# Attention values with rounded parts: 128-column products, and the halves added at the output

## The chip, the cores and the metric

The kernel runs on one core of one Trainium2 chip. The metric is the device time of one execution in microseconds (us). Engines are named as the profile names them: PE (matrix products), PEld (its weight loads), DVE (vector), ACT (scalar and functions), POOL (GpSimd), SP (here only DMA issue).

## The reference, cut to what matters

Two blocks of a network on 512 tokens of width 1024, all in float32: a block with a state-space branch, an attention branch and an MLP, then a gated-MLP layer and a second attention layer. Both attention layers are banded, with 16 query heads of width 64 on 4 key/value heads, blocks of 128 queries, and a sink logit per head. In the first a query block sees the block before, its own and the next (384 keys), in the second the block before and its own (256 keys):

```python
m = max(logits.max(-1), sink)
p = exp(logits - m)
out = (p @ v) / (p.sum(-1) + exp(sink - m))
```

## The kernel before, in words

The weights come as 66 panels of 1024 x 512 (P_... numbers a panel, O_... its output). Each is split into a rounded part w_hi (ACT, `make_hi`, L259) and the rest w_lo (POOL, L263), both of type float32r; activations are split in the same way, and a product of float32 accuracy is three float32r products: hi by hi, hi by lo, lo by hi. `main_step` (L300) gives, for one k of 8 and each m of four banks mb[m], these three products of 512 columns. At k = 0 it waits, bank by bank, until the result of the panel before has been taken from mb[m] (semaphore `bank_free`).

The attention (class `Attention`; att1 with 384 keys, att2 with 256) runs underneath such panels. Each has two halves, j = 0 and 1, of eight heads t = 0 to 7 with four query blocks c = 0 to 3. A half is a query panel (`query_panel`, which makes q and k parts and the logits of head 0), then the gate panel, during which the heads are worked off: in `heads`, step (t, m) of PE is

- before its main products: `pe_turn_p` (L789), the transposes of the probabilities of head t-1, block m, into an aux bank (ab),
- the three main products of k = t, bank m,
- after them: `pe_values` (L802), probabilities by values of head t-1, block m, into ab[3]; then `pe_logits` (L772 and L773) of head t+1, block m.

A block c has two or three key blocks of 128 in att1 (2, 3, 3, 2) and one or two in att2 (1, 2, 2, 2). Each is one product for values, of type float32, which the chip does in two instructions. The logits of a head go alternately to ab[0] and ab[1]; those of head 0 have other banks in att1.

The other engines follow in written order. ACT: `act_turned` (L880) copies the turned probabilities from the aux bank to SBUF (pt), `act_exp` (L850) makes probabilities from lg to pr, one sink exp a head (L854), one `make_hi` a head. DVE: `dve_logits` (L819) adds the bias and takes the maximum, from the logit bank to lg; `dve_den` (L889, L891) makes the reciprocal of the denominator; `dve_out` (L897) multiplies ab[3] by it into o (o1 or o2) and signals `att_out`, for which the next head's first values wait.

Where a half ends, DVE takes the four banks of the gate panel (L2162 in att1: adds the gate bias into gt; L2280 in att2: copies to zt), each signalled with bank_free, and then does den and out of head 7. On PE, head 7's turn and values are four steps of their own in att1 (`attention`), without main products between them. In att2 they lie in k = 0 of the next panel (`last_head`, and for j = 1 the output panel P_BO, line 1937). Two more things hang on output 7 in att2: DVE's gate (L2285, L2287) makes the final o, and `op_o2` (L372) transposes it on PE, under the next query panel after k = 3 for j = 0, and under P_BO after k = 2 for j = 1. `ch` is a chain on DVE: the instruction signals its end and DVE waits for that.

Of the kernel before, what the change touches and what calls it, by code (L numbers as in the profile page):

```python
# [18 lines left out]
F32 = mybir.dt.float32  # L19
# [72 lines left out]
def two_blocks(nc, d, out):  # L92
    ctx = ExitStack()
    with ctx:
# [70 lines left out]
        v_sb = at("v_sb", R0 + 24 * KB, [P, NT, 256])  # L165
# [11 lines left out]
        pr = [at("pr0", B0 + 18 * KB, [P, NT, 384]), at("pr1", B0 + 48 * KB, [P, NT, 384])]  # L177
        pt = [at("pt0", R0 + 20 * KB, [P, 384]), at("pt1", R0 + 22 * KB, [P, 384])]
        lg2 = [at("lg2a", B0 + 12 * KB, [P, NT, 256]), at("lg2b", B0 + 20 * KB, [P, NT, 256])]
        pr2 = [at("pr2a", B0 + 16 * KB, [P, NT, 256]), at("pr2b", B0 + 24 * KB, [P, NT, 256])]  # L180
# [494 lines left out]
        v_turned, v_in = sem("v_turned"), sem("v_in")  # L675
# [3 lines left out]
        p_turned, p_in, values, att_out = sem("p_turned"), sem("p_in"), sem("values"), sem("att_out")  # L679

        class Attention:
# [3 lines left out]
            def __init__(self, i, width, o, sink, lg, pr):  # L685
                self.lg, self.pr = lg, pr
# [22 lines left out]

            def act_v(self, eng):  # L710
                for j in range(2):
                    eng.wait_ge(v_turned, self.b + j + 1)
                    eng.activation(v_sb[:, :, j * P:j * P + P], ab[j][:, :].rearrange("p (c n) -> p c n", c=NT),
                                   ACT.Copy).then_inc(v_in, 1)
# [37 lines left out]
            def pe_logits(self, eng, j, t, c, og):  # L752
# [7 lines left out]
                if t == 0 and self.w == 384:  # L760
                    if c == 0:
                        eng.wait_ge(biased, one_up(j * 32 + self.b * 32))
                        eng.wait_ge(p_in, one_up(j * 32 + self.b * 32))
                        eng.wait_ge(att_out, one_up(j * 8 + self.b * 8))
                elif c >= 2 or t > 0:
                    eng.wait_ge(biased, one_up(n - 1))
                else:
                    eng.wait_ge(biased, one_up(j * 32 + self.b * 32))
# [6 lines left out]
            def logit_bank(self, t, c):  # L775

                return ab[c if t == 0 and self.w == 384 else c % 2]

            def turned_bank(self, t, c):

                return ab[1 if t == 7 and c % 2 else 2]

            def pe_turn_p(self, eng, j, t, c):
# [3 lines left out]
                eng.wait_ge(p_in, one_up(n - 1 if t == 7 and c else n))  # L787
                for b in range(nb):
                    x = eng.transpose(self.turned_bank(t, c)[:, b * P:b * P + P], self.pr[t % 2][:, c, off + b * P:off + b * P + P], ident)  # L789
                x.then_inc(p_turned, 1)  # L790

            def pe_values(self, eng, j, t, c):
                half = t // 4
                n = j * 32 + (self.b * 32 + t * 4 + c)
                lo, nb, off = self.span(c)
                if c == 0:
                    if t == 0:
                        eng.wait_ge(v_in, self.b + 2)
                    eng.wait_ge(att_out, one_up(j * 8 + (self.b * 8 + t)))
                eng.wait_ge(p_in, one_up(n + 1))  # L800
                for b in range(nb):
                    x = eng.matmul(ab[3][:, c * HP:c * HP + HP], pt[c % 2][:, b * P:b * P + P],  # L802
                                   v_sb[:, lo + b, bass.ds(j * P + half * HP, HP)],
                                   start=(b == 0), stop=(b == nb - 1))
                x.then_inc(values, 1)

            def dve_logits(self, eng, j, t, cs=range(NT)):
                for c in cs:
# [3 lines left out]
                    if c == 0:  # L812

                        eng.wait_ge(exp_done, one_up(j * 32 + (self.b * 32 + max(t - 1, 0) * 4)))
                        if t >= 2:
                            eng.wait_ge(sink_exp, j * 8 + (self.b * 8 + t - 1))
# [23 lines left out]
            def act_exp(self, eng, j, t, cs):  # L840
# [3 lines left out]
                if 0 in cs:  # L844
                    eng.wait_ge(den_done, one_up(j * 8 + (self.b * 8 + max(t - 1, 0))))
                    eng.wait_ge(values, one_up(j * 32 + (self.b * 32 + max(t - 1, 0) * 4)))
# [1584 lines left out]
```

## Time and profile before

| | |
|---|---|
| median of 3 runs | 1859.57 us (1858.75 to 1859.9) |
| the profiled execution's own time | 1861.01 us |
| its span | 1859.1 us |
| busy in the span | PE 97%, DVE 45%, ACT 46%, POOL 45% |
| att1: query panels and heads | about 562 to 741 us from the start |
| att2: query panels and heads | about 1641 to 1815 us |

The span is what the trace covers, from the first to the last instruction; the time holds in addition what lies around it. Starts in the rows are us from the start of the span. In a timeline row stand the start, the duration, engine, line, operation, output<-input, the shape and how many were merged, then in brackets the idle time before it and who ended it. Matmuls are pipelined: the duration of one overlaps the next, so two starts are compared, not durations.

### The profile page before, as it was taken

The page shows a single profiled execution, that of the slowest core. Times are in us where ns is not written, and L with a number is a line of the kernel's source. Part 1 is how long each engine was busy: PE and PEld are TensorE (multiplying, and loading weights), DVE is VectorE, ACT ScalarE, POOL GpSimd, SP SyncE. Part 2 cuts the span into 40 slices and gives each one's busy share as a digit, 9 for nine tenths or more (in the row PEclk, how much of TensorE's full clock was granted, in tenths as well). Part 3 has the DMA queues.
Part 4 walks back from the last instruction along what each step waited for, and adds up shares of the span by engine and source line. Part 5 has one row for each costly group of instructions (what it writes and reads, how often), then busy time and mean ns, then how long its engine had stood idle before and what let it go on. Part 6 is the DMA issues. An engine that isn't in the chain of part 4 may idle for free.

```text
span 1859.1 us, 26998 instructions
## 1 busy us (share of the span) xinstructions
PE 1810.3 (97%) x9064; PEld 1505.4 (81%) x9064; DVE 832.6 (45%) x1384; ACT 848.2 (46%) x1795; POOL 834.8 (45%) x598
## 2 busy tenths in 40 slices
PE   8999999999999999999999999999999999999998
PEld 7788888887888888888888888877888888887776
DVE  4688888888304443235430033050253311534644
ACT  4655555554325655324442244253533332456652
POOL 4654555577353132435444444445454444442322
PEclk9999999999999999999999999999999999999999
DMA  5732121222133121423233333324232223221211
GB/s 175 138 90 69 56 68 56 60 64 57 57 102 120 52 79 51 132 89 102 83 98 102 91 102 91 102 81 159 81 108 80 85 86 102 80 71 57 63 40 57
DMA packets 46223, 159.85 MB, mean 86 GB/s; under 512 B 4763, under 2 KB 7195, under 8 KB 45884
## 3 DMA queue, kind: packets, MB, share of 16 engines
q1 hardware_dynamic: 38592, 140.53, 24.7%
q10 hardware_dynamic: 7548, 18.20, 4.0%
q8 instruction: 54, 0.88, 0.2%
q14 instruction: 29, 0.24, 0.0%
HBM read 152.42 MB, written 6.29 MB: 85 GB/s over the span
## 4 chain that ended last, share of the span: by engine, by line
PE 81%; DVE 8%; issue 4%; ACT 4%; POOL 1%; DMA 1%; DVEq 0%; ACTq 0%; POOLq 0%
PE main L300 60%; PE main L328 4%; PE aux L802 4%; PE aux L656 2%; PE main L1800 2%; PE aux L789 2%; DVE u_acc L2002 1%; PE aux L772 1%; PE aux L372 1%; DVE x_res L564 1%; PE aux L773 1%; DVE y_all L2080 1%; PE aux L1888 1%; PE aux L647 1%; ACT w_hi L259 1%
## 5 line engine op out<-in xcount | busy, mean ns | idle before, releaser
L263 POOL TENSOR_TENSOR w_lo<-raw,w_hi 128x512 fp32r<-128x512 f32 x504 | 700.7, 1397 | 895.0 <-ACT w_hi L259 883.1
L259 ACT ACTIVATE w_hi<-raw 128x512 fp32r<-128x512 f32 x486 | 304.5, 630 | 696.7 <-PE main L300 683.7
L300 PE MATMUL main<-w_hi,a_hi 128*128 128x512 f32 x736 | 304.2, 413 | 2.3 <-ACT vv L1547 1.5
L300 PE MATMUL main<-w_hi,a_lo 128*128 128x512 f32 x736 | 288.1, 391 | 0.0
L300 PE MATMUL main<-w_lo,a_hi 128*128 128x512 f32 x736 | 287.3, 390 | 0.0
L300 PE MATMUL main<-a_hi,w_hi 128*128 128x512 f32 x576 | 231.2, 401 | 1.6 <-ACT u_raw L1296 1.6
L300 PE MATMUL main<-a_hi,w_lo 128*128 128x512 f32 x576 | 225.2, 391 | 0.0
L300 PE MATMUL main<-a_lo,w_hi 128*128 128x512 f32 x576 | 224.9, 390 | 0.0
L300 PEld LDWEIGHTS main<-w_hi,a_lo 128*128 128x128 f32 x736 | 138.1, 188 | 30.3
L300 PEld LDWEIGHTS main<-w_hi,a_hi 128*128 128x128 f32 x736 | 138.5, 188 | 28.4 <-ACT vv L1547 1.9
L300 PEld LDWEIGHTS main<-w_lo,a_hi 128*128 128x128 f32 x736 | 138.8, 189 | 23.0
L300 PE MATMUL main<-w_hi,f_hi 128*128 128x512 f32 x352 | 138.6, 394 | 1.5 <-DVE f_lo L385 1.5
L300 PE MATMUL main<-w_hi,f_lo 128*128 128x512 f32 x352 | 137.2, 390 | 0.0
L300 PE MATMUL main<-w_lo,f_hi 128*128 128x512 f32 x352 | 137.1, 389 | 0.0
L300 PEld LDWEIGHTS main<-a_hi,w_hi 128*128 128x128 f32 x576 | 108.5, 188 | 25.0 <-issue 2.8
L300 PEld LDWEIGHTS main<-a_hi,w_lo 128*128 128x128 f32 x576 | 108.4, 188 | 23.7
L300 PEld LDWEIGHTS main<-a_lo,w_hi 128*128 128x128 f32 x576 | 108.6, 188 | 22.3
L2002 DVE SCALAR_TENSOR_TENSOR u_acc<-u_raw,par,u_acc 128x510 f32<-128x510 f32 (+1 forms) x128 | 112.3, 946 | 2.4 <-DVE hst L2059 2.3
L802 PEld LDWEIGHTS aux<-v_sb,pt 128*128 128x128 f32 x544 | 70.3, 190 | 39.5 <-ACT pt L880 22.1
L802 PE MATMUL aux<-v_sb,pt 128*128 (+1 forms) x544 | 83.0, 278 | 4.5 <-ACT pt L880 2.9
L880 ACT ACTIVATE pt<-aux 128x256 f32<-128x256 f32 (+2 forms) x128 | 50.7, 397 | 75.5 <-PE aux L789 73.1
L300 PEld LDWEIGHTS main<-w_hi,f_hi 128*128 128x128 f32 x352 | 66.1, 188 | 15.1 <-DVE f_lo L385 1.8
(320 smaller groups left out, 3111.7 us busy)
## 6 DMA issues: line engine op xcount, KB each, us to landing
raw<-w_stream_in SPq DMA_DIRECT2D x264, 512.0 KB, 3.6
x_res<-x_in ACTq DMA_DIRECT2D x8, 512.0 KB, 5.1
rel_rows<-rel_row ACTq DMA_DIRECT2D x1, 4096.0 KB, 44.3
bias<-rel_rows ACTq DMA_DIRECT2D x2, 1536.0 KB, 8.3
out<-x_res SPq DMA_DIRECT2D x4, 512.0 KB, 2.7
bgate<-b_gate_in ACTq DMA_DIRECT2D x4, 256.0 KB, 5.8
ln_g<-ln_g_in ACTq DMA_DIRECT2D x1, 1024.0 KB, 4.7
ln_b<-ln_b_in ACTq DMA_DIRECT2D x1, 1024.0 KB, 6.8
```

The source lines that it names most:

```text
L259: eng.activation(w_hi[:, k, :], raw[:, k, :], ACT.Copy).then_inc(hi_done, 1)
L263: eng.tensor_tensor(w_lo[:, k, :], raw[:, k, :], w_hi[:, k, :].bitcast(F32), ALU.subtract).then_inc(lo_done, 1)
L300: mm = eng.matmul(mb[m][:, :], lhs, rhs, start=(first and k == 0 and n == 0), stop=(last and k == KT - 1 and n == 2))
L328: mm = eng.matmul(out, lhs, rhs, start=(first and k == 0 and n == 0), stop=(last and k == KT - 1 and n == 2))
L372: t = eng.transpose(b[:, m * P:m * P + P], self.src[:, m, c:c + P], ident)
L564: eng.scalar_tensor_tensor(x_res[:, m, :], self.fb[:, m, :], small[:, self.s + m:self.s + m + 1], x_res[:, m, :], ALU.mult, ALU.add).then_ ...
L656: x = eng.matmul(ab[c // 2][:, (c % 2) * GW + r * HP:(c % 2) * GW + r * HP + HP], dmat[r][:, dr, c * P:c * P + P], xdt[:, dr, c, r * HP:r ...
L789: x = eng.transpose(self.turned_bank(t, c)[:, b * P:b * P + P], self.pr[t % 2][:, c, off + b * P:off + b * P + P], ident)
L802: x = eng.matmul(ab[3][:, c * HP:c * HP + HP], pt[c % 2][:, b * P:b * P + P], v_sb[:, lo + b, bass.ds(j * P + half * HP, HP)], start=(b == ...
L880: eng.activation(pt[c % 2][:, 0:nb * P], self.turned_bank(t, c)[:, 0:nb * P], ACT.Copy).then_inc(p_in, 1)
L1800: mm = pe.matmul(mb[m][:, :], lhs, rhs, start=False, stop=(k == KT - 1 and n == 2))
L2002: ins = dve.scalar_tensor_tensor(acc, u_raw[:, m, i0:i0 + o1_ - o0], tap(m, k), acc, ALU.mult, ALU.add)
```

## The change

Values v are split into a rounded part and the rest when they are turned: ACT writes the rounded part (`act_v`), DVE the rest (new `dve_v`), side by side in v_hl, 64 + 64 columns per head and key block. Turned probabilities are split too: ACT's copy now writes float32r (p_hi), and DVE writes the rest (new `dve_rest`, PSUM minus p_hi, into p_lo). Per key block `pe_values` gives one product of p_hi with both parts of v (128 columns), and one of p_lo with the rounded part of v (64 columns) that adds onto the first half. So ab[3] holds 128 columns per block: `dve_out` adds the two halves with a reduce of 512 elements to 256, chained, and then multiplies in place by the reciprocal.

Around it: probabilities overwrite the logits in lg (pr is gone). Values lag one step: after step (t, m) come the values of block m-1, and at m = 0 those of (t-2, 3). Logits of all heads but head 0 use the one bank ab[0]; turned probabilities alternate between ab[1] and ab[2], and a turn waits for the rest of two blocks before (`p_rest`). Output t-2 is made on DVE at c = 0 of the loop's head t. In both attentions head 7's turn and values lie in k = 0 of the next panel, the last values in k = 1; DVE does its rests between taking the banks (`dve_last`).

```diff
             def pe_values(self, eng, j, t, c):
...
                 for b in range(nb):
-                    x = eng.matmul(ab[3][:, c * HP:c * HP + HP], pt[c % 2][:, b * P:b * P + P],
-                                   v_sb[:, lo + b, bass.ds(j * P + half * HP, HP)],
-                                   start=(b == 0), stop=(b == nb - 1))
+                    eng.matmul(ab[3][:, c * P:c * P + P], self.p_hi[c % 2][:, b * P:b * P + P],
+                               v_hl[:, head, lo + b, :].rearrange("p o n -> p (o n)"), start=(b == 0), stop=False)
+                eng.wait_ge(p_rest, one_up(n + 1))
+                for b in range(nb):
+                    x = eng.matmul(ab[3][:, c * P:c * P + HP], self.p_lo[c % 2][:, b * P:b * P + P],
+                                   v_hl[:, head, lo + b, 0:HP].rearrange("p o n -> p (o n)"), start=False, stop=(b == nb - 1))
                 x.then_inc(values, 1)
...
             def logit_bank(self, t, c):
-                return ab[c if t == 0 and self.w == 384 else c % 2]
+                if t == 0:
+                    return ab[c if self.w == 384 else c % 2]
+                return ab[0]
...
+            def dve_rest(self, eng, j, t, c):
+                n = j * 32 + (self.b * 32 + t * 4 + c)
+                lo, nb, off = self.span(c)
+                eng.wait_ge(p_in, one_up(n + 1))
+                eng.tensor_tensor(self.p_lo[c % 2][:, 0:nb * P], self.turned_bank(c)[:, 0:nb * P],
+                                  self.p_hi[c % 2][:, 0:nb * P].bitcast(F32), ALU.subtract).then_inc(p_rest, 1)
...
-                eng.tensor_tensor(o, ab[3][:, 0:NT * HP].rearrange("p (c n) -> p c n", c=NT),
-                                  small[:, 56:60].unsqueeze(2).broadcast_to((P, NT, HP)), ALU.mult).then_inc(att_out, 1)
-                eng.wait_ge(att_out, one_up(q + 1))
+                ch(eng.tensor_reduce(o, ab[3][:, :].rearrange("p (c a n) -> p c n a", c=NT, a=2), AX.X, ALU.add))
+                eng.tensor_tensor(o, o, small[:, rc:rc + NT].unsqueeze(2).broadcast_to((P, NT, HP)), ALU.mult).then_inc(att_out, 1)
...
             def dve_heads(self, eng, ch, j):
                 for t in range(8):
-                    if t:
-                        self.dve_den(eng, ch, j, t - 1)
-                    if t < 7:
-                        self.dve_logits(eng, j, t + 1)
-                    if t:
-                        self.dve_out(eng, j, t - 1)
+                    for c in range(NT):
+                        if t:
+                            self.dve_rest(eng, j, t - 1, c)
+                            if c == 0 and t >= 2:
+                                self.dve_out(eng, ch, j, t - 2)
+                        if t < 7:
+                            self.dve_logits(eng, j, t + 1, [c])
+                        if t and c == 1:
+                            self.dve_den(eng, ch, j, t - 1)
+
+            def dve_last(self, eng, ch, j, c):
+                self.dve_rest(eng, j, 7, c)
+                if c == 0:
+                    self.dve_out(eng, ch, j, 6)
+                    self.dve_den(eng, ch, j, 7)
...
                     def after(m):
-                        if t:
-                            att.pe_values(pe, j, t - 1, m)
+                        if t and m:
+                            att.pe_values(pe, j, t - 1, m - 1)
+                        elif t >= 2:
+                            att.pe_values(pe, j, t - 2, 3)
                         if t < 7:
                             att.pe_logits(pe, j, t + 1, m, og)
...
                 for m in range(NT):
                     wait_full(dve, j * 2 + (P_QZ + 1), j * 2 + (O_QZ + 1), m)
                     dve.tensor_copy(zt[:, m, :], mb[m][:, :]).then_inc(bank_free, 1)
-                att2.dve_den(dve, ch, j, 7)
-                att2.dve_out(dve, j, 7)
+                    att2.dve_last(dve, ch, j, m)
+                att2.dve_out(dve, ch, j, 7)
```

In att1 the last loop is changed in the same way, around the add into gt. `dve_den` keeps its reciprocal in one of two places, so that output t-1 can come after den t. ACT copies turned block c, then makes the exp of block c, in turn for the four blocks, and then `make_hi`. PE's loop over the two halves of att1 is written out, so that the second query panel can take head 7 of the first half in its k = 0.

## Rows read from the trace of the kernel before

**Rows 1.** The page: busy time per engine, and the chain by engine.

```profile
PE 1810.3 (97%) x9064; PEld 1505.4 (81%) x9064; DVE 832.6 (45%) x1384; ACT 848.2 (46%) x1795; POOL 834.8 (45%) x598
...
PE 81%; DVE 8%; issue 4%; ACT 4%; POOL 1%; DMA 1%; DVEq 0%; ACTq 0%; POOLq 0%
```

**Rows 2.** Timeline of PE, a head of the second attention: start, us.

```profile
1696.65 0.40 PE L300 MATMUL main<-w_hi,a_lo 128*128 128x512 f32 x1
1697.16 0.43 PE L802 MATMUL aux<-v_sb,pt 128*128 128x64 f32 x2
...
1697.55 0.28 PE L773 MATMUL aux<-k_ll1b,q_hl1b 128*128 128x128 f32 x1
1697.66 0.41 PE L789 MATMUL aux<-const,pr2b 128*128 128x128 f32 x2
...
1703.20 0.40 PE L300 MATMUL main<-w_hi,a_lo 128*128 128x512 f32 x1
```

**Rows 3.** Timeline of PE, a head of the first attention.

```profile
604.61 0.40 PE L300 MATMUL main<-w_hi,a_lo 128*128 128x512 f32 x1
...
606.87 0.88 PE L802 MATMUL aux<-v_sb,pt 128*128 x6
607.56 0.42 PE L772 MATMUL aux<-k_hh1a,q_hl1a 128*128 128x384 f32 x1
...
612.52 0.40 PE L300 MATMUL main<-w_hi,a_lo 128*128 128x512 f32 x1
```

**Rows 4.** Groups by line and shape, weight loads of values and logits: mean ns.

```profile
L802 PEld LDWEIGHTS aux<-v_sb,pt 128*128 128x128 f32 x544 | 70.3, 190 | 39.5 <-ACT pt L880 22.1 <-DVE o L897 11.9 <-issue 5.5
...
L773 PEld LDWEIGHTS aux<-k_ll,q_hl 128*128 128x128 f32 x64 | 12.2, 190 | 0.6
```

**Rows 5.** Groups by line and shape on DVE: busy us, mean ns of one.

```profile
L2080 DVE TENSOR_TENSOR y_all<-y_all,off_t 128x256 f32 x36 | 23.9, 663 | 3.2 <-DVE off_t L2070 1.0
...
L819 DVE CUSTOM_DVE_ANT_0 lg<-aux,bias,ssq 128x384 f32<-128x384 f32 x32 | 19.6, 617 | 38.5 <-PE aux L773 38.5
...
L897 DVE TENSOR_TENSOR o<-aux,small 128x256 f32<-128x256 f32 x32 | 13.5, 421 | 26.0 <-PE aux L802 26.0
```

**Rows 6.** Timeline of PE, ends of a half in the first and second attention.

```profile
640.82 0.39 PE L789 MATMUL aux<-const,pr 128*128 128x128 f32 x2
...
646.02 0.50 PE L300 MATMUL main<-a_hi,w_hi 128*128 128x512 f32 x1
...
1719.80 0.39 PE L789 MATMUL aux<-const,pr2a 128*128 128x128 f32 x2
...
1720.73 0.66 PE L802 MATMUL aux<-v_sb,pt 128*128 128x64 f32 x4
1722.75 0.30 PE L789 MATMUL aux<-const,pr2b 128*128 128x128 f32 x1 [1.36 <-issue]
...
1727.80 0.48 PE L300 MATMUL main<-a_hi,w_hi 128*128 128x512 f32 x1
```

**Rows 7.** Timeline of DVE, the end of a half in the second attention.

```profile
1721.50 0.42 DVE L897 TENSOR_TENSOR o<-aux,small 128x256 f32<-128x256 f32 x1 [4.03 <-PE aux L802]
1721.96 2.48 DVE L2280 COPY zt<-main 128x512 f32<-128x512 f32 x4
...
1724.55 0.18 DVE L891 RECIPROCAL small<-small 128x4 f32<-128x4 f32 x1
```

**Rows 8.** Timeline of PE, first values of the second attention.

```profile
1677.55 0.41 PE L802 MATMUL aux<-v_sb,pt 128*128 128x64 f32 x2 [1.52 <-ACT pt L880]
```

**Rows 9.** Timeline of PE under the last half's output panel.

```profile
1814.19 1.09 PE L372 MATMUL aux<-const,o 128*128 128x128 f32 x8 [1.46 <-DVE o L2287]
```

**Rows 10.** Busy us by window: PE, PEld, DVE, ACT, POOL, PE clock, DMA.

```profile
1642.50:1646.00 3.50, 1.23 (x12) 1.06 (x11) 0.00 (x0) 2.76 (x6) 2.54 (x2) 1.00 0.16 37
1646.00:1649.40 3.40, 3.40 (x14) 2.92 (x13) 0.02 (x1) 2.55 (x6) 0.00 (x0) 0.50 0.47 154
...
1720.50:1724.00 3.50, 2.14 (x15) 1.59 (x14) 2.46 (x5) 1.09 (x3) 1.26 (x1) 1.00 0.01 2
```

More of the change, by code:

```diff
@@ L885, in dve_den @@
                 sm, es = small[:, 36 + 4 * (t % 2):40 + 4 * (t % 2)], small[:, 44 + 4 * (t % 2):48 + 4 * (t % 2)]
-                dn, rc = small[:, 52:56], small[:, 56:60]
+                dn, rc = small[:, 52:56], small[:, self.per_den(t):self.per_den(t) + 4]
                 eng.wait_ge(sink_exp, q + 1)
@@ L1149, in _ @@
                 load_quarter(sp, 0, q)
-            for semaphore in (logits, biased, values, exp_done, den_done, p_in, att_out, f_ready, sp_y, yt_turned, yt_ready, z_gate, sp_full):
+            for semaphore in (logits, biased, values, exp_done, den_done, p_in, p_rest, att_out, f_ready, sp_y, yt_turned, yt_ready, z_gate, sp_full):
                 sp.sem_inc(semaphore, 1)
@@ L1789, in query_panel @@
                         main_step(pe, p, k, h, l, True, og, before=last_head[0], after=last_head[1])
+                    elif k == 1 and last_head is not None:
+                        main_step(pe, p, k, h, l, True, og, after=lambda m: last_head[2]() if m == 0 else None)
                     else:
@@ L1824, in first_logits, with last_of @@
                     att.pe_logits(pe, j, 0, c, og)
-            def attention(att, op, j, p, og):
-                query_panel(p, og, op, lambda m: first_logits(att, j, m, og))
-                heads(att, op, j, p, og)
-                att.pe_turn_p(pe, j, 7, 0)
-                for c in range(NT):
-                    if c < 3:
-                        att.pe_turn_p(pe, j, 7, c + 1)
-                    att.pe_values(pe, j, 7, c)
-            with pe.Fori(0, 2) as j:
-                attention(att1, ao, j, j * 2 + P_QG, j * 2 + O_QG)
-            panel(P_GA, O_GA, ao, False)
+            def last_of(att, j):
+                return att.pe_last_before(pe, j), att.pe_last_after(pe, j), lambda: att.pe_values(pe, j, 7, 3)
+            query_panel(P_QG, O_QG, ao, lambda m: first_logits(att1, 0, m, O_QG))
+            heads(att1, ao, 0, P_QG, O_QG)
+            query_panel(P_QG + 2, O_QG + 2, ao, lambda m: first_logits(att1, 1, m, O_QG + 2), last_head=last_of(att1, 0))
+            heads(att1, ao, 1, P_QG + 2, O_QG + 2)
+            before, after, later = last_of(att1, 1)
+            for k in range(KT):
+                if k == 0:
+                    main_step(pe, P_GA, k, *ao(k), False, O_GA, before=before, after=after)
+                elif k == 1:
+                    main_step(pe, P_GA, k, *ao(k), False, O_GA, after=lambda m: later() if m == 0 else None)
+                else:
+                    main_step(pe, P_GA, k, *ao(k), False, O_GA)
             pe.wait_ge(att_out, one_up(NQ))
@@ L1936, in _ @@
                 if k == 0:
-                    main_step(pe, P_BO, k, *o_at(k), False, O_BO, before=lambda m: att2.pe_turn_p(pe, 1, 7, m),
-                              after=lambda m: att2.pe_values(pe, 1, 7, m))
+                    main_step(pe, P_BO, k, *o_at(k), False, O_BO, before=before2, after=after2)
+                elif k == 1:
+                    main_step(pe, P_BO, k, *o_at(k), False, O_BO, after=lambda m: later2() if m == 0 else None)
                 else:
```

112 lines of the change are left out of this document (68 added, 44 removed).

## The prediction

> **What bounds the kernel now.** I read the page's busy shares first and the chain that ended last second: the reader is to see that PE is busy for 97% of the span and carries 81% of the chain [rows 1]. A microsecond in which PE waits is a microsecond of run time; the other engines count only through what they make PE wait for. The change touches the two attention stages, each in two halves (j = 0, 1). So the third view is PE's order inside one head, where I call turn, three main products, values and logits of one query block c a step. Every head holds one short wait, at c = 0: main products follow each other by 0.23 us, but in the second attention values start 0.51 us after the third, 0.28 lost [rows 2]; in the first it is less. A head lasts 6.55 us in the second attention (1696.65 to 1703.20) and 7.91 in the first (604.61 to 612.52) [rows 2, 3]. The fourth view is the place where a half ends, with its DVE rows [rows 6, 7]: there DVE frees all four main banks in one go, 2.48 us for the four, and only then does the last head's sums.
>
> **PE's own work.** Old values: two fp32 instructions per key block, six of them (three blocks) in 0.69 us, 0.112 each [rows 3]. New: one of 128 columns with the rounded part and one of 64 with the rest, also two per block. The nearest row is a rounded logits product of 128 columns: its successor starts 0.11 us later [rows 2], and weights load in 190 ns for both kinds [rows 4]. So count and pitch stay and PE saves nothing: 0. Bounds: with loads cheaper by half, 544 x 0.057 = 31 us less; with instructions as far apart as main products, 0.23, 64 us more. I take 0, by the row of the same kind.
>
> The Trainium skill, page "TensorE: Matmul & The Clock Gate", section on weight-path perf modes, says that fast weight load is on for 128 weights whose type isn't FP32. If it counted the rounded type as such, the new products would load faster and 31 us would go; the 190 ns of rows 4 speak against it.
>
> **DVE's new work.** Per block the rest (PSUM minus rounded part): 0.42 us for 256 columns, as o from aux; for 384 a little under lg's 0.617, I take 0.55 [rows 5]. The output was one multiply, 0.42. It becomes a reduce over 512 elements in PSUM, 0.68 (the pace of zt's copies there is 0.62, the last one's own end adds 0.06) [rows 7], 0.03 for the wait between (1721.50 + 0.42 to 1721.96), and a multiply of 256 elements in SBUF. No reduce stands in the trace: below, 0.42 if its output of 256 set it; above, 1.33, twice y_all's 0.66. The multiply: below 0.42 as from PSUM, above y_all's 0.66 [rows 5]. I take 0.68 + 0.03 + 0.42 = 1.13 us (the rows from PSUM are the nearest), ends 0.87 and 2.02.
>
> **Inside a head (t = 2 to 6).** The output of head t-2 now waits for values(t-2, 3), which PE gives in step c = 0 of the next head; DVE starts 0.38 us after the start of the last values product (1721.50 against 1720.73 + 3 x 0.112 + 0.05) [rows 6, 7]. Second attention, from the start of that step: turn 0.06, main 0.78, last values product at 1.17, +0.38 = 1.55, +1.13 = 2.68. The step itself lasts 1.51. PE's values(t-1, 0) in the next step could go at 0.87 into it and go at 2.68 - 1.51 + 0.05 = 1.22: 0.35 lost. Behind the output on DVE stands the bias of logits(t+1, 0), 0.36 us more; logits have only bank 0 now, so logits(t+1, 1) wait another 0.14. Steps: 1.51 + (1.48 + 0.49) + 1.67 + 1.65 = 6.80 against 6.55: five heads, two halves, **+2.5**. First attention by the same count: output ends at 1.63 + 1.13 = 2.76, the step lasts 1.66, the waits are 0.15 and 0.07, the head 7.92 against 7.91: **0**. The other rests are hidden by the lag of one step: turn to ACT 0.53, copy 0.49, DVE 0.55 end 1.6 us into a step of 1.9 to 2.2, and their values come a step later. ACT issues copies and exps in another order, the same rows.
>
> **First and last heads.** With one bank the logits of head 1 wait for each bias: in the first attention 1.5 us by the start of head step (1, 0), of which the first values' wait on ACT and the lag give 1.0 back: +0.5 per half, **+1.0**. In the second attention, j = 0, values(0, 0) waited 1.52 us for ACT's copy [rows 8]; it goes, against bank waits: -0.9; in j = 1 there is no such wait: +0.3; **-0.6**. Head 7 has no logits to cover the output: +0.3 per half in the second attention, **+0.6**.
>
> **The end of a half** is the large term. After the gate panel DVE now goes bank by bank: free bank m, rest(7, m), and at m = 0 also output 6 and den 7. PE waits for bank m+1 ahead of the turn of step m+1, and rest(7, m) needs PE's turn of step m. So bank m+1 comes a full circle PE, ACT, DVE after step m began, where before DVE had freed all four beforehand.
> - Entry, from the turn of (6, 3): ACT's copy from 0.42 to 0.80, rest to 1.29, bank 0 to 1.93, PE at 2.0.
> - Step 0: output starts at 1.55 (first attention 1.63), +1.13, den 0.41 (a small sum and a reciprocal of 0.18, with their gaps), bank 1 0.72 [rows 7], PE +0.07: 3.88 (3.95).
> - Steps 1 and 2, second attention: 0.42 to ACT, 0.38, 0.06, rest 0.42, bank 0.65, 0.07: 2.0 each. First, with three blocks: 0.53, 0.49, 0.06, 0.55, 0.65, 0.07: 2.35 each.
> - Step 3: 1.36 (1.61), and values(7, 3) under the next k: 0.43 (0.41).
> Second attention: 2.0 + 3.88 + 2.0 + 2.0 + 1.36 + 0.43 = 11.67 against 1719.80 to 1727.80, 8.00 [rows 6]: +3.7, twice **+7.3**. First: 2.0 + 3.95 + 2.35 + 2.35 + 1.61 + 0.41 = 12.67 against 640.82 to 646.02, 5.20, and twelve main products at 0.23: 7.98: +4.7, twice **+9.4**.
>
> **Behind it.** Before 1814.19 PE waited 1.46 us for the last half's o [rows 9]; that hangs on output 7, which now ends 2.53 us after the last step against 0.75: +1.8, of which 0.43 is counted already: **+1.35**, and +0.15 for j = 0. The two more DVE instructions for v's rest (0.68 each; ACT keeps its two) stand beside the query panel, 22 us of main products: 0; without this cover 1.4 a stage. The bias DMA behind ACT's tanh moves with PE and is needed some 14 us after: 0.
>
> **Sum:** 2.5 + 0 + 1.0 - 0.6 + 0.6 + 7.3 + 9.4 + 1.5 = **+21.7 us**. The profiled execution took 1861.0 us (span 1859.1 and 1.9 around it): 1882.7 with the change. It stood 1.4 above the median of 1859.57, so I give **1881**.
>
> **Rivals.**
> (a) The ends cost nothing: DVE frees each bank inside PE's own step and only old waits go. It decides at 1.4 us, the length of such a step; I count 3.9 for the first and 2.0 after. Gains: at most 0.28 in seven heads of four halves (7.8), 1.36 before 1722.75 in each second-attention half (2.7), 1.0 in each first: about 12, **1848**. For it: DVE is busy for 45% [rows 1]. Against it: one output of 0.42 ahead of the copies held PE for that 1.36 already [rows 6, 7]. 5%.
> (b) Reduce or multiply is slower (POOL's w_lo beside it, as y_all's rows may show): +0.3 for each of 29 outputs on the path, +9: **1890**. 14%.
> (c) The clock falls at the ends. Before 1646 PE was busy for 1.23 us of 3.5, and in the next stretch the granted clock was 0.50, the level of 1.2 GHz; with 2.14 us of 3.5 it stayed at 1.00, that of 2.4 GHz [rows 10]. The new steps 0 have some 1.3 busy of 3.9. One fall costs some 1.5 us (an estimate: seven main products at twice 0.23); four, +6: **1887**. 12%. The same page of the Trainium skill says in its part on the clock gate that pauses between bursts bring the clock down; the row of 1646 agrees, that of 1720.5 does not.
> (d) Rounded parts load faster, 31 us against the 21 lost: **1850**. 2%.
> (e) The circles are shorter (a reduce at 0.42, waits absorbed elsewhere): +8 to +14, about **1870**, 12%; down to no change 3%.
>
> **Numbers.** The forecast, 1875 to 1886, has 52%. For 8 in 10 I reach past (e)'s middle and past (b): 1868 to 1893. A measurement of this kernel tells 0.2% (3.7 us) from no change. Faster is (a) and (d), 0.07; same 0.03; slower 0.90.
>
> **What would show it.** Right: PE idle some 2.5 us ahead of the turn of m = 1 and 0.6 to 0.8 us ahead of m = 2 and 3 at each of four ends; the first k of the next panel about 10 us long; heads of 6.8 and 7.9 us; values instructions still 0.112 us apart; reduce rows near 0.68 us. Wrong: heads of the second attention under 6.5 us, values instructions under 0.1 us apart, or DVE freeing banks without gaps. A granted clock of 0.50 after an end would be (c).

## The result and the profile after

The changed kernel takes **1881.36 us** (median of 4 runs, 1879.29 to 1882.18) against 1859.16 for the kernel before on the same chip: ratio 1.0118, 95% interval 1.010 to 1.0135. The forecast was 1881.0. The total agrees to 0.4 us; the terms behind it do not, and most of what follows is about that. The profiled execution took 1881.75 us with a span of 1879.9, 20.8 more than before.

The page, busy time and chain, against [rows 1]:

```profile
PE 1816.9 (97%) x9064; PEld 1523.9 (81%) x9064; DVE 906.2 (48%) x1548; ACT 844.8 (45%) x1795; POOL 835.0 (44%) x598
...
PE 81%; DVE 9%; issue 4%; ACT 3%; POOL 1%; DMA 1%; DVEq 0%; ACTq 0%; POOLq 0%
```

PE has the same 9064 instructions. DVE has 164 more (four v rests, 128 probability rests, 32 reduces) and 74 us more work, but its share of the chain grew by only 1 point in 100. Where it grew has to be looked for.

The timeline of PE over one head of the second attention (turn to turn, 1699.58 to 1705.98), against [rows 2]:

```profile
1699.58 0.41 PE L806 MATMUL aux<-const,lg2a 128*128 128x128 f32 x2
1699.75 0.48 PE L299 MATMUL main<-w_hi,a_hi 128*128 128x512 f32 x1
...
1700.29 0.40 PE L299 MATMUL main<-w_hi,a_lo 128*128 128x512 f32 x1
1700.74 0.33 PE L820 MATMUL aux<-v_hl,pt 128*128 128x128 f32 x1
1700.90 0.25 PE L824 MATMUL aux<-v_hl,pt 128*128 128x64 f32 x1
...
1703.87 0.33 PE L820 MATMUL aux<-v_hl,pt 128*128 128x128 f32 x2
1704.04 0.36 PE L824 MATMUL aux<-v_hl,pt 128*128 128x64 f32 x2
...
1705.98 0.29 PE L806 MATMUL aux<-const,lg2b 128*128 128x128 f32 x1
```

At 1700.74 the first values of a head start 0.45 us behind the third main product, 0.22 more than the 0.23 between main products (for the output; in all this step lasts 0.36 longer than in a kernel without that wait, below). In the other three steps there is nothing: 1703.87 is 0.23 behind the main product at 1703.64. The head lasts 6.40 us, less than the 6.55 of before, where the forecast had 6.80. In the first attention it lasts 7.44 (603.64 to 611.08), against 7.91.

The groups by line and shape of values and of the new DVE work, against [rows 4, 5]:

```profile
L820 PEld LDWEIGHTS aux<-v_hl,pt 128*128 128x128 f32 x272 | 50.9, 201 | 20.8 <-DVE o L940 10.7
L824 PEld LDWEIGHTS aux<-v_hl,pt 128*128 128x128 f32 x272 | 43.2, 203 | 0.3
...
L910 ACT ACTIVATE pt<-aux 128x384 fp32r<-128x384 f32 x32 | 15.7, 491 | 33.9 <-PE aux L806 33.9
L917 DVE TENSOR_TENSOR pt<-aux,pt 128x256 fp32r<-128x256 f32 x80 | 33.9, 424 | 21.2 <-ACT pt L910 17.0
L917 DVE TENSOR_TENSOR pt<-aux,pt 128x384 fp32r<-128x384 f32 x32 | 17.8, 555 | 8.4 <-ACT pt L910 8.0
L939 DVE TENSOR_REDUCE o<-aux 128x256 f32<-128x512 f32 x32 | 22.1, 692 | 20.8 <-PE aux L824 20.8
L940 DVE TENSOR_TENSOR o<-o,small 128x256 f32<-128x256 f32 x32 | 13.6, 425 | 1.1
```

Every duration that the trace of before did not have came out as sized: rest 0.42 and 0.56 us (0.42, 0.55), reduce 0.69 (0.68), multiply 0.42 (0.42). The weight loads show something else: before, values' loads stood idle 22.1 us for ACT's copy [rows 4]; here the largest entry is 10.7 us for the output, and ACT's copy names none.

The end of the first half in the first attention: PE's timeline, cut to the turns, and the chain of waits through the same stretch (start, us, what):

```profile
640.29 0.41 PE L806 MATMUL aux<-const,lg 128*128 128x128 f32 x2 [0.29 <-issue]
644.01 0.55 PE L806 MATMUL aux<-const,lg 128*128 128x128 f32 x3 [2.25 <-DVE gt L2223]
646.33 0.90 PE L806 MATMUL aux<-const,lg 128*128 128x128 f32 x3 [0.70 <-DVE gt L2223]
649.44 0.69 PE L806 MATMUL aux<-const,lg 128*128 128x128 f32 x2
```

```profile
641.79 0.70 DVE o L939
642.52 0.04 DVE o L940
642.55 0.31 issue
642.86 0.17 DVE small L931
643.05 0.19 DVE small L933
643.26 0.70 DVE gt L2223
```

The circle is the one forecast: last values of head 6, reduce, multiply, denominator, reciprocal, and only then bank 1. The steps are 3.72 and 2.32 us (forecast 3.95, 2.35), in the second attention 3.61 and 1.97 (3.88, 2.0). But the third step is 3.11 us, without any wait: the turn at 646.33 alone takes 0.90. The windows (PE, PEld, DVE, ACT, POOL busy, granted clock, DMA), against [rows 10]:

```profile
640.30:645.50 5.20, 2.95 (x19) 2.58 (x19) 2.87 (x7) 0.90 (x3) 1.29 (x1) 1.00 0.30 102
645.50:655.80 10.30, 9.60 (x35) 8.41 (x35) 3.42 (x8) 5.97 (x11) 0.00 (x0) 0.50 0.31 89
...
737.70:748.00 10.30, 10.07 (x35) 8.84 (x36) 3.42 (x7) 3.46 (x7) 1.27 (x1) 0.51 0.09 25
...
1734.40:1741.20 6.80, 6.38 (x24) 5.48 (x23) 2.47 (x5) 2.89 (x7) 0.00 (x0) 0.50 0.02 5
...
1819.70:1823.10 3.40, 3.22 (x12) 2.60 (x11) 1.89 (x4) 0.67 (x2) 0.00 (x0) 0.50 0.04 17
```

Behind the waits the granted clock is 0.50, 1.2 GHz, at all four ends, for about 31 us in all. Before there was no such stretch at any of them. The third step in the second attention lasts 2.47 and 2.24 us, against 2.0 forecast, for the same reason.

Last, DVE's gate in the second attention, from which the final o comes, behind j = 0:

```profile
1743.19 0.68 DVE L2347 SCALAR_TENSOR_TENSOR gt<-gt,zt 128x512 f32<-128x512 f32 x1
1743.91 0.69 DVE L2349 TENSOR_TENSOR o<-o,gt 128x512 f32<-128x512 f32 x1
1744.52 1.78 DVE L2347 SCALAR_TENSOR_TENSOR gt<-gt,zt 128x512 f32<-128x512 f32 x1
1746.34 1.67 DVE L2349 TENSOR_TENSOR o<-o,gt 128x512 f32<-128x512 f32 x1
```

```profile
1752.75 1.09 PE L371 MATMUL aux<-const,o 128*128 128x128 f32 x8 [3.08 <-DVE o L2349]
```

The same instruction takes 0.69 or 1.6 to 1.8 us. Four of the eight are long here, one of eight before, and PE waits 3.08 us for the last. Part of this comes back: the kernel before waited 1.66 us at its next turn of o, and the changed kernel has no wait there. The row of the kernel before:

```profile
1741.53 0.66 PE L372 MATMUL aux<-const,o 128*128 128x128 f32 x4 [1.66 <-DVE o_lo L385]
```

**Where the 20.8 us went.** The same PE instructions were followed in both traces; the table has after minus before over each stretch, summed over the four halves:

| stretch | forecast | measured |
|---|---|---|
| first heads (up to and with the loop's head 1) | +0.4 | -0.5 |
| loop's heads 2 to 6 | +2.5 | -6.2 |
| head 7 and the ends, up to k = 2 of the next panel | +17.3 | +25.2 |
| behind them | +1.5 | +4.2 |
| outside the attention stages | 0 | -1.9 |
| sum | +21.7 | +20.8 |

The 1.9 us outside the attention stages are no effect of the change that a run shows. They lie where no instruction was changed, and there the trace of before, and not that of after, has a stretch at half clock (window of the kernel before):

```profile
874.60:881.40 6.80, 6.14 (x28) 6.14 (x29) 5.25 (x9) 3.04 (x8) 2.17 (x2) 0.50 0.18 37
```

Two errors of about 11 us stand against each other (-0.9, -8.7 and the -1.9 against +7.9 and +2.7). The theory to test: the **lag** saves time in every head, the **order of DVE at the ends** loses more, part of it directly and part through the clock; the split itself (its products and its rests) costs nearly nothing inside a head.

### The profile page after: what moved, and what is told of

It is laid out like the page before. It is cut to its first block, busy times and chain, and to the rows that moved or that the text cites. A ratio compares the mean times of both kernels' runs of the same rounds, so it can differ in the third digit from the quotient of the medians.

```text
span 1879.9 us, 27095 instructions
## 1 busy us (share of the span) xinstructions
PE 1816.9 (97%) x9064; PEld 1523.9 (81%) x9064; DVE 906.2 (48%) x1548; ACT 844.8 (45%) x1795; POOL 835.0 (44%) x598
## 4 chain that ended last, share of the span: by engine, by line
PE 81%; DVE 9%; issue 4%; ACT 3%; POOL 1%; DMA 1%; DVEq 0%; ACTq 0%; POOLq 0%
PE main L299 60%; PE main L327 4%; PE main L1853 2%; PE aux L655 2%; PE aux L806 2%; PE aux L820 2%; PE aux L824 1%; DVE u_acc L2062 1%; PE aux L785 1%; PE aux L371 1%; PE aux L786 1%; DVE x_res L563 1%; DVE y_all L2140 1%; PE aux L1946 1%; PE aux L646 1%
## 5 line engine op out<-in xcount | busy, mean ns | idle before, releaser
L299 PEld LDWEIGHTS main<-a_hi,w_lo 128*128 128x128 f32 x576 | 109.4, 190 | 23.8
L910 ACT ACTIVATE pt<-aux 128x256 fp32r<-128x256 f32 (+2 forms) x128 | 50.9, 397 | 100.2 <-PE aux L806 99.7
L299 PEld LDWEIGHTS main<-w_hi,f_lo 128*128 128x128 f32 x352 | 66.1, 188 | 14.0
L2262 DVE TENSOR_TENSOR relu<-relu 128x512 f32<-128x512 f32 x32 | 25.1, 840 | 108.2 <-ACT relu L1569 108.2
```

The lines of the kernel that those rows point to most:

```text
L299: mm = eng.matmul(mb[m][:, :], lhs, rhs, start=(first and k == 0 and n == 0), stop=(last and k == KT - 1 and n == 2))
L910: eng.activation(self.p_hi[c % 2][:, 0:nb * P], self.turned_bank(c)[:, 0:nb * P], ACT.Copy).then_inc(p_in, 1)
L2262: dve.tensor_tensor(relu[:, m, :], relu[:, m, :], relu[:, m, :], ALU.mult).then_inc(f_sq, 1)
```

## The experiments

Ratios are to the kernel before on the same chip.

| run | median us | ratio (95%) |
|---|---|---|
| e1_banks_first | 1859.9 | 1.0006 (0.9995 to 1.0016) |
| e2_filled | 1872.7 | 1.0064 (1.004 to 1.0087) |
| e3_fp32 | 1851.0 | 0.996 (0.9947 to 0.9974) |
| e4_fp32_no_lag | 1867.0 | 1.004 (1.0026 to 1.0054) |
| e5_split_no_lag | 1931.8 | 1.038 (1.0359 to 1.04) |
| e6_two_banks | 1856.8 | 0.9993 (0.9983 to 1.0003) |
| e7_fp32_both | 1840.9 | 0.9902 (0.9886 to 0.9919) |
| e8_early | 1846.5 | 0.9942 (0.9926 to 0.9959) |
| e10_small_rests | 1849.8 | 0.9956 (0.9939 to 0.9973) |
| e11_o_later | 1853.2 | 0.9973 (0.9964 to 0.9983) |
| e12_all | 1835.4 | 0.9881 (0.9864 to 0.9897) |
| e13_split_all | 1846.2 | 0.9923 (0.9909 to 0.9936) |

**e1: DVE frees all four banks first**, as before the change; the rests, output 6 and den 7 follow.

```diff
                 for m in range(NT):
                     wait_full(...)
                     dve.tensor_tensor(gt[:, m, :], mb[m][:, :], bgate[:, :], ALU.add).then_inc(bank_free, 1)
+                for m in range(NT):
                     att1.dve_last(dve, ch, j, m)
```

The same in the second attention, behind the copies to zt.

> At the end of a half VectorE takes all four main banks first and then does the four rests, output 6 and den 7; nothing else differs from the changed kernel. Theory (PE waits for the circle PE, ACT, DVE before each bank, and the clock falls because of it): the idle times of about 2.3 and 0.7 us ahead of the turns of m = 1, 2, 3 go or fall below 1 us, the granted clock stays at 1.00 at the four ends, each end is 3 to 7 us shorter, the kernel takes 1856 to 1862 us. Rival (the ends are long because DVE has more to do in all, so the same work only moves): ends shorter by under 1 us each, 1877 us or more.

Measured: 1859.9, 21.5 us less, as the theory had it. DVE's timeline and PE's first turn behind it:

```profile
639.18 2.47 DVE L2223 TENSOR_TENSOR gt<-main,bgate 128x512 f32<-128x512 f32 x4
...
641.26 0.55 PE L806 MATMUL aux<-const,lg 128*128 128x128 f32 x3
```

The turn at 641.26 has no wait; the first three steps are 1.30, 2.30 and 1.67 us (3.72, 2.32, 3.11) and the clock stays at 1.00 at both ends of the first attention. From head 7's loop step to k = 2 of the next panel 17.0, 17.0, 15.4 and 15.4 us pass, where the changed kernel took 23.8, 24.1, 20.3 and 18.6: 22 us less. This one reordering on DVE takes away all of the loss that can be measured: the interval of e1 holds 1. In the second attention 3.4 us at 0.50 remain behind the waits for the final o (from 1734.4).

**e2: PE is kept busy in the waits of the ends** with products that nobody reads (9, 2 and 2 of 512 columns into ab[0], behind steps 0, 1 and 2); the first of them wait until DVE has read the last logits from ab[0]. All of DVE's order stays.

```diff
                         self.pe_values(eng, j, 6, 3)
+                        eng.wait_ge(biased, one_up(j * 32 + self.b * 32 + 32))
+                    for _ in range((9, 2, 2, 0)[m]):
+                        eng.matmul(ab[0][:, :], w_hi[:, 0, 0:P], w_hi[:, 0, :], start=True, stop=True)
```

> The changed kernel with idle products put into the wait of the end of a half: nine of 512 columns into a free bank after the values of step 0, two after those of steps 1 and 2. Bank waits stay as they are. Theory (a part of an end's length is the clock that falls to 0.50 after the long wait): the granted clock stays at 1.00 at the ends, the steps after the second take 2.3 and 1.6 us instead of 3.1 and 2.7 in the first attention, and the kernel gets 8 to 11 us faster, 1870 to 1873 us. Rival (the clock does not matter since PE waits anyway): within 2 us of 1881.

Measured: 1872.7, 8.7 us less than the changed kernel with 52 products more. The windows of the same stretches:

```profile
640.30:645.50 5.20, 5.09 (x28) 3.87 (x26) 3.39 (x8) 0.79 (x2) 0.87 (x1) 1.00 0.32 104
645.50:655.80 10.30, 10.13 (x55) 8.38 (x55) 6.43 (x11) 6.52 (x12) 1.52 (x1) 1.00 0.47 151
```

Steps 0 and 1 keep their 3.72 and 2.32 us (the circle is DVE's), but step 2 is 2.32 and these stretches run at full clock. The ends shrink by 3.7, 4.0, 2.0 and 0.3 us. So of the 25.2 us at the ends about 10 are the clock's, and without it 15.2 are left, against 17.3 forecast.

**e3: the split taken out**: float32 values and probabilities, no rests, one multiply for the output; order, lag, banks and the places of head 7 as changed. (What is left out is the split, so this computes the same by float32 products.)

```diff
-                    eng.matmul(ab[3][:, c * P:c * P + P], self.p_hi[c % 2]..., v_hl[:, head, lo + b, :]..., start=(b == 0), stop=False)
-                eng.wait_ge(p_rest, one_up(n + 1))
-                for b in range(nb):
-                    x = eng.matmul(ab[3][:, c * P:c * P + HP], self.p_lo[c % 2]..., v_hl[:, head, lo + b, 0:HP]..., start=False, ...)
+                    x = eng.matmul(ab[3][:, c * HP:c * HP + HP], self.p_hi[c % 2]..., v_sb[:, lo + b, ...], start=(b == 0), ...)
```

> The changed kernel with the split taken out: probabilities and values in float32, one product of 64 columns per key block as before, no rests, one multiply at the output; order, lag, banks and the place of head 7 stay as in the changed kernel. Theory (heads got shorter because values lag a step, so their weights are no longer awaited from ACT): heads stay at 7.5 us or less in the first attention and at 6.3 to 6.4 in the second, against 7.91 and 6.55 before; with the rests gone the ends need only output and den before the second bank. 1853 to 1860 us. Rival (heads got shorter because rounded products are quicker): heads return to 7.75 us or more and 6.5, 1862 us or more.

Measured: 1851.0, faster than both kernels and 2 us under the range expected. Its heads have steps of 1.43, 1.39, 1.60, 1.60 us in the second attention, the changed kernel's 1.42, 1.76, 1.60, 1.60; in the first 1.60, 1.82, 2.04, 1.83 and 1.60, 1.99, 2.05, 1.82. Three of four steps are equal, so two products of 128 and 64 columns take what two float32 instructions take. The fourth holds the late output: 0.17 and 0.36 us a head are the price of the split inside it.

**e4 and e5: the lag undone**, in the float32 and in the split kernel.

```diff
-                        if t and m:
-                            att.pe_values(pe, j, t - 1, m - 1)
-                        elif t >= 2:
-                            att.pe_values(pe, j, t - 2, 3)
+                        if t:
+                            att.pe_values(pe, j, t - 1, m)
```

The same in `pe_last_after`, and output t-1 at the end of the loop's head t.

> This is the kernel of the third run (the split taken out: float32 probabilities and values, one multiply at the output, 1851.0 us), with the lag undone as well: the values of a block stand in the block's own step again, behind the three main products, and output t-1 stands at the end of the loop's head t, as before the change. Banks, the order of ACT and DVE and the places of head 7 stay changed. What is left out: the split. Theory (the lag is what shortened the heads, because the values' weight loads waited for ACT's copy in nearly every step): heads go back to about 7.9 us in the first attention and 6.5 in the second, so +0.6 for 12 heads and +0.5 for 12: +13 us on 1851.0, about 1864, less up to 3 where the ends are one step shorter. Rival (the banks or the interleaved order of ACT and DVE made the gain): heads stay at 7.3 and 6.0 or below, time 1848 to 1851.

> The changed kernel with the lag alone undone, as in the run beside it; split, rests, banks and last heads stay. Values then wait in their own step for ACT's copy and, at the second product, for DVE's rest of 0.42 to 0.56 us. Theory (the lag covers copy and rest, and the split costs time only where that cover is gone): heads of 7.9 + about 4 x 0.15 = 8.5 us in the first attention (7.46 with the lag) and 6.5 + 0.6 = 7.1 in the second (6.39): +12.5 and +8.5, so 1881 + 21 = about 1902, less up to 5 where the last steps of the ends are shorter. Rival (the values' first products, which need only the copy, cover the rest, so that the split is free without a lag too): heads as in the float32 run without lag, about 7.9 and 6.5, time 1888 to 1892.

Measured: e4 1867.0 (+16.0 on e3; 13 expected), with heads of 7.91 and 6.55 us, the two numbers of the kernel before to the last digit, with other banks and another order of ACT and DVE. The gain in the heads is the lag (of values and output) and nothing else. The groups of the values' weight loads, first in e4, then in a float32 kernel that keeps the lag (e7, below):

```profile
L815 PEld LDWEIGHTS aux<-v_sb,pt 128*128 128x128 f32 x544 | 71.6, 192 | 37.9 <-ACT pt L898 22.8 <-DVE o L922 11.9 <-issue 2.6
```

```profile
L821 PEld LDWEIGHTS aux<-v_sb,pt 128*128 128x128 f32 x544 | 80.5, 190 | 11.3
```

e5 took 1931.8, 30 us more than its theory, and 50 more than with the lag: heads of 9.60 and 8.24. The theory had only the rest in the way; PE's timeline shows the output too:

```profile
619.64 0.44 PE L820 MATMUL aux<-v_hl,pt 128*128 128x128 f32 x2 [0.74 <-DVE o L937]
```

Here reduce and multiply of output t-1 stand behind the bias of the last logits, and the next head's first values wait for them; step 0 has 2.71 us against 1.87 in e4. At the ends e5 has 13.7 us at half clock twice. My price for it was wrong, its sign not: the split without the lag costs 65 us (1931.8 against 1867.0), with it 30 (1881.4 against 1851.0), and with the order of e1 and two banks 16 (e6 below against e7).

**e6: two banks for the logits of head 1** in the first attention (ab[0], ab[3]), on top of e1. **e7: the same in the float32 kernel** (split left out).

```diff
+                if t == 1 and self.w == 384:
+                    return ab[3 if c % 2 else 0]
                 return ab[0]
```

> The kernel of the first run (DVE takes all four banks first, 1859.9 us), and in the first attention the logits of head 1 go alternately to two banks, ab[0] and ab[3], instead of all to ab[0]. Theory: the 1.23 us that PE waits for DVE ahead of head 1's second logits at each of the two starts shrinks to about the 0.19 of the kernel before, and each start is 1.0 to 1.5 us shorter: 1859.9 - 2.5 = 1857.4. Rival: the wait is for the pace of DVE's bias instructions (4 of 0.62 to 0.80 us for head 0 and 4 for head 1) and only moves to a later step: no change, 1859.9. Either way the first full head begins at 589.0 less the gain.

> Split taken out, all four banks taken first, and two banks for head 1's logits in the first attention: the float32 kernel with the lag and with both mends. What is left out: the split of probabilities and values. Theory (gains of separate places add): 1851.0, less about 0.85 us at each of four ends (steps of 6.1 and 5.5 us to about 5.2 and 4.6), less about 1.2 at each of two starts: 1851.0 - 3.4 - 2.4 = about 1845. Rival (DVE holds the ends of the float32 kernel only in the output, and the banks taken first put that output 1 us later, where the aux transposes wait for it): ends unchanged, 1848.5.

Measured: e6 1856.8 (-3.1). PE's second logits of head 1, in e1 and in e6:

```profile
585.99 0.45 PE L785 MATMUL aux<-k_hh,q_hl 128*128 128x384 f32 x1 [1.24 <-DVE small L854]
```

```profile
586.70 0.45 PE L787 MATMUL aux<-k_hh,q_hl 128*128 128x384 f32 x1 [0.19 <-DVE small L860]
```

1.05 us less wait at each start; the theory held. e7 1840.9, 4 us below its theory: the ends gave 1.75 and 1.87 us each, not 0.85 (steps 4.38 and 3.61 us, from 6.11 and 5.48). I had taken e1's steps as the floor, which still hold the late output.

**e8: the last values of a head ahead of the main products** of step (t, 0), and so at the ends, on top of e6.

```diff
                     def before(m):
                         if t:
                             att.pe_turn_p(pe, j, t - 1, m)
+                        if t >= 2 and m == 0:
+                            att.pe_values(pe, j, t - 2, 3)
```

> The kernel with banks first and two banks for head 1's logits (1856.8 us), and the last values of a head, which output t-2 waits for, stand ahead of the three main products of step (t, 0), behind the turn, instead of behind them; the same at the ends (values (6,3) at k = 0, values (7,3) at k = 1). Theory (what is left of the split inside a head is the reduce, which makes output t-2 late at step c = 1): output starts 0.65 us earlier and the wait goes: step c = 1 falls from 1.99 to 1.82 and from 1.76 to 1.40 us as in the float32 kernel, heads to 7.29 and 6.03; 12 x 0.17 + 12 x 0.36 = -6.4, and the 0.5 to 0.7 us before values (7,0) at four ends, -2.4: about 1848. Rival (the rest of block 3 is not ready at the turn, 1.6 us after its own, and PE waits there instead): step c = 0 longer by what c = 1 gains, 1856 to 1860.

Measured: 1846.5 (-10.3): step 1 falls from 1.99 to 1.83 and from 1.76 to 1.40, heads are 7.29 and 6.03, the float32 kernel's. With this order the split costs nothing inside a head. 0.57 and 0.64 us before values (7,0) stay at the ends (0.60 and 0.67 in e6); there the theory missed. In its place the loop's head 7 fell by 0.33 and 0.47 us, and the two waits for the final o from 3.06 and 2.77 to 1.30 and 1.96. (The step from k = 1 to 2 fell from 3.28 to 2.85 too, but only because values (7,3) now stand ahead of it: each whole end is 0.32 or 0.47 shorter, no more than its head 7.)

**e10: POOL's w_lo cut to 8 of 512 columns** behind P_KV2, on top of e6. (The other columns of these rests are left out.)

> The kernel with banks first and two banks (1856.8 us), and in the panels behind P_KV2 POOL makes only 8 of the 512 columns of each w_lo. What is left out: the rest of the other columns of these weights (their old content is multiplied); PE's work is the same. Theory (DVE's gate instructions of 0.69 us take 1.6 to 1.8 us because POOL's w_lo runs beside them, and this delays o ahead of the transposes): all 16 gate instructions at 0.69, the 3.06 us of PE ahead of the first transposes under the second query panel go to about 0, the 2.77 us under the output panel to about 1.7: -3 to -4, about 1853. Rival (the long ones are long for another reason, DMA or PE's own reads): durations and waits unchanged, 1856.8.

Measured: 1849.8 (-7.0). The groups of the gate instructions, in the changed kernel and in e10:

```profile
L2347 DVE SCALAR_TENSOR_TENSOR gt<-gt,zt 128x512 f32<-128x512 f32 x8 | 8.8, 1095 | 0.0
L2349 DVE TENSOR_TENSOR o<-o,gt 128x512 f32<-128x512 f32 x8 | 7.5, 931 | 0.3
```

```profile
L2357 DVE SCALAR_TENSOR_TENSOR gt<-gt,zt 128x512 f32<-128x512 f32 x8 | 5.5, 686 | 0.0
L2359 DVE TENSOR_TENSOR o<-o,gt 128x512 f32<-128x512 f32 x8 | 5.5, 692 | 0.3
```

All sixteen are short, and PE's transposes behind j = 0 have no wait (3.06 in e6), and those behind j = 1 wait 1.70 (2.77). The gain is twice the theory's. The waits give 4.1 us of it. The rest fits the clock: e6 has 3.4 us at 0.50 behind each of the two waits, e10 behind neither. These are single traces. Behind j = 0, e6 and then e10:

```profile
1728.00:1731.40 3.40, 3.40 (x12) 2.82 (x11) 3.31 (x5) 1.19 (x2) 0.00 (x0) 0.50 0.47 151
```

```profile
1728.00:1731.40 3.40, 3.40 (x21) 2.85 (x19) 2.69 (x5) 1.43 (x3) 0.27 (x1) 1.00 0.37 119
```

The Trainium skill, page "GPSIMD Engine Reference", section 1 (specifications), says that GpSimd's SBUF interfaces are shared with VectorE, with contention where a DVE instruction has two SBUF inputs. The gate instructions have two, and this case agrees: 0.69 us in e10, up to 1.78 with full w_lo beside them.

**e11: transposes of o later**, by one pass of 12 main products, on top of e6.

```diff
             def under_q1(m):
-                if m < 2:
-                    op_o2.pe(pe, [m + 2])
+                if m == 0:
+                    turn_first_o2()
+                if m == 1:
+                    op_o2.pe(pe, [2, 3])
```

> The kernel with banks first and two banks (1856.8 us), and the transposes of the first half's o in the second attention come 12 main products later (tiles 0 and 1 behind the first pass of the second query panel, 2 and 3 behind the second). Theory (the 3.06 us wait is only a due date set too early): -2.7 us, 1854; the clock, at 0.50 for 3.4 us at that place in some profiles, stays at 1.00 there, up to -1.5 more. Rival (the transposes' copies then collide with ACT's and DVE's part in the first logits of the half, and those wait): unchanged, 1856.8.

Measured: 1853.2 (-3.6). The wait goes from 3.06 to 0.38 us; 0.77 us before the first logits are new.

**e12 and e13: all four together** (e1, e6, e8, e11). e12 was made from the float32 kernel by a slip, so its expectation speaks of another kernel than the one that ran, and the split is left out in it. e13 is the split kernel.

> All of it for the split kernel: banks first, two banks, early last values, later transposes of o. Theory (they are separate places and add): 1856.8 - 9 - 2.7 = about 1845, clearly under the kernel before (1858.5). Rival: they share slack (each moves the same later wait): 1848 to 1852.

> The run e12_all was made from the float32 kernel (split taken out) by a slip, so its 1835.4 us is the float32 kernel with all four mends, not the split one its expectation speaks of. This is the split kernel with all four: banks first, two banks for head 1's logits, early last values, later transposes of o. Theory (the mends add, and what is left of the split is what it costs at the four ends, where PE waits about 1.7 to 2.4 us more per end for the reduce and the rests: 1846.5 against 1840.9 in the float32 kernel with the same first two mends and no output wait): 1846.5 - 3.6 (what the later transposes gave alone) = 1843, under the kernel before by 0.8%. Rival (with all mends the split's waits at the ends fall into slack, and it costs nothing): 1835 to 1838.

Measured: float32 1835.4, split 1846.2. Both beat both kernels, by 1.2% and 0.8% of the kernel before. e13 is 3 us above its theory and 8 above the rival's upper end. By ratio, it is 0.2% below e8 and their intervals overlap: whether the later transposes add anything once the values are early is open. The split's rest price is 0.4% (0.9923 against 0.9881). It sits at the ends, whose seven steps from the loop's head 7 on take 6.51 + 5.28 us (e8) against 5.97 + 4.43 (e12) in the first attention, and 5.70 + 4.59 against 4.97 + 3.66 in the second: 6.1 us of the 10.7 in four ends. The two profiled executions are only 8.5 us apart; where the rest between the medians lies is open. PE's waits at one of them, e13:

```profile
1709.64 0.30 PE L810 MATMUL aux<-const,lg2b 128*128 128x128 f32 x1 [0.51 <-issue]
1712.64 0.33 PE L826 MATMUL aux<-v_hl,pt 128*128 128x128 f32 x1 [0.64 <-DVE o L948]
```

## Why the prediction was right in its total and wrong in its terms

- **PE's own work, 0**: held. Values' instructions are 0.11 us apart and their loads last 201 ns (190 before); e8's heads equal the float32 kernel's within 0.02 us. The rival of faster loads (d) is out.
- **DVE's new work**: held, each within 0.01 us.
- **Inside a head, +2.5**: wrong in sign, and by the prediction's own list of signs wrong: it named heads of the second attention under 6.5 us, and they are 6.40. The new wait was there (step 1 longer by 0.17 and 0.36; I had 0.22 and 0.49 by the same count). What failed is the sentence that every head holds one short wait, at c = 0. I had read one step of rows 2 and put rows 4 beside it only for the 190 ns; its idle column, 22.1 us for ACT's copy and 11.9 for the output over some 100 steps, says that the copy was late in nearly every step: some 90 of these waits last 0.20 to 0.32 us each. The lag removes just that (e4). Measured -6.2 for heads 2 to 6.
- **First and last heads, +0.4 and +0.6**: near. The starts are longer by 1.5 us each in the first attention and 1.2 in the second, and the loop's head 1, which has no values any more at its first step, is shorter by 1.4, 1.4, 2.3 and 0.9. Together that is +0.1, +0.1, -1.1 and +0.3 by half, against +0.5, +0.5, -0.9 and +0.3. The loop's head 7, up to its last turn, is 0.3 shorter in the first attention and 0.1 longer in the second, where I had 0 and +0.3.
- **The ends, +16.7**: the mechanism and the circle held step by step: entry 2.01 for 2.0, step 0 3.72 and 3.61 for 3.95 and 3.88, step 1 2.32 and 1.97 for 2.35 and 2.0, and e1 removes it. At full clock the sum is near: without the 10 us of the clock (e2) the stretch of the table is 15.2 us longer than before, against 17.3. What failed is that the sum was made at full clock. Rival (c) had the mechanism and was priced at 6 us, seven main products a fall; e2 shows 9 to 10, because two of the falls last 10.2 us. I had given it 12%, as it was a rival and not a term; it came true at all four places.
- **Behind it, +1.5**: output 7 was late as counted, but behind j = 0 three more gate instructions fell beside POOL's w_lo and took 1.0 us longer each: +3.3, of which 1.9 came back at the next turn of o. Behind j = 1 only one is long, as before, and there another 3.4 us at half clock came instead (from 1833.4): +2.8. Rival (b) spoke of POOL, but reduce and multiply stayed at 0.69 and 0.42, as w_lo hardly ran beside them. In e5 it did, and there (b) is half right: the reduce kept 0.69, four multiplies took 1.12 to 1.13. Rival (a) needed DVE to free banks in a step of 1.4 us; e1 is what that would have been, 1859.9 and not 1848.

So the total is right by luck. It rests on errors that cancel: -9.6 us in the heads and -1.9 outside them, +10.6 at and behind the ends. The chance of 52% for the forecast was for a reason that holds only in part.

## What to carry to other kernels

Read the idle column of a group over all its instructions before saying how often a wait occurs: one step of a timeline shows a wait that looks like nothing, and a hundred of them are what a change is worth. When DVE has results to clear and sums to make, clear first what PE waits for; here one such reordering was worth 21.5 us, about as much as the change had cost (22.2). A wait of PE of the size seen here, 2 to 3 us, should be priced together with what the clock may do behind it, and a delay on DVE with what POOL will be doing at the new time.

## What the runs showed of the hardware

- Two waits of PE, 2.25 and 0.70 us within 5.2, were followed by up to 10.2 us at half clock although PE was busy for 9.6 of the 10.3 us of that stretch; the same order of work with the waits filled stayed at 1.00 (e2). A single wait of 3.06 us had 3.4 us at 0.50 behind it (e6), none without the wait (e10).
- Such a fall is not certain. Behind its wait of 3.08 us the changed kernel stayed at 1.00 (row below). The wait of 2.27 us ahead of the turn of v, the same in all kernels, had a stretch at 0.50 behind it in 8 of the 14 traces and none in 6. So one trace doesn't tell whether a change brings or spares a fall; e2 does by its median.

```profile
1752.80:1756.20 3.40, 3.40 (x19) 2.95 (x20) 3.27 (x6) 1.09 (x2) 0.00 (x0) 1.00 0.45 154
```

- DVE instructions of 512 elements with both inputs in SBUF, 0.69 us alone, took 1.63 to 1.78 us when POOL's two-input subtract ran beside them for 1.1 us or more: +1.0 us each. One that had 0.61 us of it beside its end kept 0.68. The rest and bias instructions, which read PSUM, show no such spread (0.42 and 0.48 us with it and without), nor does the reduce (0.69 in e5 with it beside). The multiply of the output reads SBUF alone, and in e5:

```profile
655.87 1.13 DVE L937 TENSOR_TENSOR o<-o,small 128x256 f32<-128x256 f32 x1
```

- A float32 product of 64 columns (two instructions) and the pair of rounded products of 128 and 64 columns take the same 0.22 us per key block.
